# A decoder trunk on one core: the activations' blocks side by side, 16 bytes in turn, and one pass over each

## Time and profile before

| | us |
|---|---|
| median of 3 runs (lowest to highest) | 1007.06 (1006.73 to 1007.34) |
| the profiled execution | 1007.63 |
| its span, first to last instruction | 1005.8 |
| PE busy | 993.8 |
| DVE busy | 721.1 |
| ACT busy | 510.8 |
| POOL busy | 122.6 |

### The profile page before, as it was taken

The page is one execution under the profiler, slowest core; times in us unless marked ns, Lnnn a source line. Parts: engine busy times, 40 slices in busy tenths (PEclk is TensorE's granted clock), DMA queues, the critical chain, the costliest instruction groups (busy, mean ns, idle before and its releaser), DMA issues.

```text
span 1005.8 us, 19130 instructions
## 1 busy us (share of the span) xinstructions
PE 993.8 (99%) x7932; PEld 977.8 (97%) x7932; DVE 721.1 (72%) x1077; ACT 510.8 (51%) x743; POOL 122.6 (12%) x136
## 2 busy tenths in 40 slices
PE   8999999999999999999999999999999999999997
PEld 7999999999999999999999999999989999999986
DVE  5855657689899866557697565667897998866543
ACT  5643445465456543445565444445867766544340
POOL 2000002320002000003220000134152420000000
PEclk9999999999999999999999999999999999999999
DMA  9966656637762866556639665555355747866531
GB/s 249 263 194 181 176 159 179 192 93 209 232 177 81 242 199 181 168 164 183 198 89 259 179 185 156 172 168 161 85 148 145 201 116 234 254 196 197 184 132 42
DMA packets 324264, 176.60 MB, mean 176 GB/s; under 512 B 6658, under 2 KB 320048, under 8 KB 324176
## 3 DMA queue, kind: packets, MB, share of 16 engines
q1 hardware_dynamic: 323664, 174.15, 59.6%
q0 software_dynamic: 480, 1.15, 0.4%
q10 hardware_dynamic: 32, 0.07, 0.0%
HBM read 174.29 MB, written 1.05 MB: 174 GB/s over the span
## 4 chain that ended last, share of the span: by engine, by line
PE 90%; DVE 4%; DMA 1%; ACT 1%; issue 1%; POOL 1%; SPq 0%; POOLq 0%; DVEq 0%; ACTq 0%
PE bank L1318 23%; PE bank L1315 23%; PE bank L1320 23%; PE bank L1334 3%; PE bank L1335 3%; PE bank L1336 3%; PE bank L1475 2%; PE bank L1476 2%; PE bank L1474 2%; PE bank L1359 2%; PE bank L1360 2%; PE bank L1361 2%; DVE weights_lo L823 1%; DMA raw_weights<-in_ffn_w_in_dram 1%; DVE rms L1223 1%
## 5 line engine op out<-in xcount | busy, mean ns | idle before, releaser
L464 ACT ACTIVATE weights_hi<-raw_weights 128x1024 fp32r<-128x1024 f32 x335 | 353.7, 1059 | 403.9 <-PE bank L1320 286.5
L823 DVE TENSOR_TENSOR weights_lo<-raw_weights,weights_hi 128x1024 fp32r<-128x1024 f32 x334 | 417.0, 1255 | 196.0 <-ACT weights_hi L464 194.8
L1315 PE MATMUL bank<-x_hi,weights_hi 128*128 128x272 f32 (+1 forms) x1584 | 225.7, 285 | 0.5 <-ACT consts L628 0.5
L1318 PE MATMUL bank<-x_hi,weights_lo 128*128 128x272 f32 (+1 forms) x1584 | 224.0, 283 | 0.0
L1320 PE MATMUL bank<-x_lo,weights_hi 128*128 128x272 f32 (+1 forms) x1584 | 223.0, 282 | 0.0
L1315 PEld LDWEIGHTS bank<-x_hi,weights_hi 128*128 128x128 f32 x1584 | 206.0, 189 | 1.1 <-ACT consts L628 0.7
L1318 PEld LDWEIGHTS bank<-x_hi,weights_lo 128*128 128x128 f32 x1584 | 204.8, 188 | 0.0
L1320 PEld LDWEIGHTS bank<-x_lo,weights_hi 128*128 128x128 f32 x1584 | 204.2, 187 | 0.0
L1320 PE MATMUL bank<-mid_lo,weights_hi 128*128 128x272 f32 x462 | 67.2, 285 | 0.0
L1318 PE MATMUL bank<-mid_hi,weights_lo 128*128 128x272 f32 x462 | 66.8, 284 | 0.0
L1315 PE MATMUL bank<-mid_hi,weights_hi 128*128 128x272 f32 x462 | 66.7, 284 | 0.0
(11 more groups left out here) (230 smaller groups left out, 1208.6 us busy)
## 6 DMA issues: line engine op xcount, KB each, us to landing
raw_weights<-in_ffn_w_in_dram SPq DMA_DIRECT2D x176, 512.0 KB, 4.6
raw_weights<-in_ffn_w_out_dram SPq DMA_DIRECT2D x70, 512.0 KB, 3.6
raw_weights<-in_conv_w_in_dram SPq DMA_DIRECT2D x24, 512.0 KB, 3.9
raw_weights<-in_gla_w_in_dram SPq DMA_DIRECT2D x24, 512.0 KB, 3.9
raw_weights<-in_ffn_w_out_dram SPq DMA_DIRECT2D x24, 384.0 KB, 3.2
raw_weights<-in_conv_w_out_dram SPq DMA_DIRECT2D x8, 512.0 KB, 4.9
raw_weights<-in_gla_w_out_dram SPq DMA_DIRECT2D x8, 512.0 KB, 5.0
x_tok<-in_x_dram SPq DMA_DIRECT2D x2, 512.0 KB, 4.9
```

The source lines that it names most:

```text
L464: nc.scalar.activation(w_hi[:, n % RING, :], raw[:, n % RAW, :], ACT.Copy).then_inc(hi_split, 1)
L823: nc.vector.tensor_tensor(w_lo[:, s, :], raw[:, n % RAW, :], w_hi[:, s, :].bitcast(F32), ALU.subtract).then_inc(lo_split, 1)
L1315: nc.tensor.matmul(into, block_of(w_hi, n, k - k0), walk(hi[:, k, cols]), start=first and k == k0, stop=False)
L1318: nc.tensor.matmul(into, block_of(w_lo, n, k - k0), walk(hi[:, k, cols]), start=False, stop=False)
```

## The change

The four-pass walk is taken from the streamed activations, and their memory is laid out so that a single pass has the same 64-byte step. An area has groups of four blocks (SIDE = 4); in a group 4 words (RUN = 4, 16 bytes) of block 0 are followed by 4 of block 1, of block 2, of block 3, and then the next 4 of block 0. `side_by_side(area)` gives a function `block(k, cols)`, which returns block k as lines of 4 words, 64 bytes from line to line. `runs(ap)` gives a contiguous row the same shape of lines of 4, so that the two sides of an instruction agree; PSUM is then written from first to last column. The engines that write hi and lo parts write them into this layout, and with the same number of elements as before. `mid_hi` and `mid_lo` become one tensor of 44 blocks. The units with 256 columns in the GLA stage, and `y`, take the layout too. The fourth FFN keeps its packed x at the same offset of 48 words, and its middle blocks are packed at 256 words without the meta tokens (`last_mid`); the weights there are streamed by rows as before. No instruction, wait or transfer is added or removed.

```diff
+    RUN, SIDE = 4, 4
...
-        x_hi_area = sb("x_hi", [P, KD, T + 16], F32R)
-        x_lo_area = sb("x_lo", [P, KD, T + 48], F32R)
-        x_hi, x_lo = x_hi_area[:, :, 0:T], x_lo_area[:, :, 0:T]
+        x_hi_area = sb("x_hi", [P, KD // SIDE, T // RUN, SIDE, RUN], F32R)
+        x_lo_area = sb("x_lo", [P, KD // SIDE, T // RUN, SIDE, RUN], F32R)
+
+        def runs(ap):
+            return ap.rearrange("p (l e) -> p l e", e=RUN)
+
+        def side_by_side(area, first=0):
+            def block(k, cols):
+                at = first + k
+                return area[:, at // SIDE, cols.start // RUN:cols.stop // RUN, at % SIDE, :]
+            return block
...
-            mid_hi = inner.enter_context(nc.sbuf_tensor("mid_hi", [P, KF, T], F32R))
-            mid_lo = inner.enter_context(nc.sbuf_tensor("mid_lo", [P, KF, T], F32R))
+            mid = inner.enter_context(nc.sbuf_tensor("mid", [P, 2 * KF // SIDE, T // RUN, SIDE, RUN], F32R))
+        mid_hi, mid_lo = side_by_side(mid), side_by_side(mid, KF)
+        mid_words = mid[:].rearrange("p g l k e -> p (g l k e)")[:, 0:2 * KF * SEQ]
+        last_mid = mid_words.rearrange("p (s k t) -> p s k t", s=2, k=KF)
...
-                nc.scalar.activation(y_hi[:, m, :], y_t[:, m % 4, :], ACT.Copy).then_inc(yhi_ready, 1)
+                nc.scalar.activation(y_hi(m, main), runs(y_t[:, m % 4, :]), ACT.Copy).then_inc(yhi_ready, 1)
...
-                    nc.vector.tensor_copy(mid_hi[:, at_t, cols], prod[:, s:s + 1, cols]).then_inc(midhi_ready, 1)
+                    if f == 3:
+                        part_hi, part_lo = runs(last_mid[:, 0, t, :]), runs(last_mid[:, 1, t, :])
+                    else:
+                        part_hi, part_lo = mid_hi(t, cols), mid_lo(t, cols)
+                    nc.vector.tensor_copy(part_hi, runs(prod[:, s, cols])).then_inc(midhi_ready, 1)
...
-                walk = by_rows if ps.shape[-1] == T else lambda ap: ap
-                into = walk(ps)
+                into = runs(ps)
...
-                        nc.tensor.matmul(into, block_of(w_hi, n, k - k0), walk(hi[:, k, cols]), start=first and k == k0, stop=False)
+                        nc.tensor.matmul(into, block_of(w_hi, n, k - k0), hi(k, cols), start=first and k == k0, stop=False)
...
-                    nc.tensor.matmul(ps, mid_hi[:, k, toks], by_rows(w_hi[:, slot, cols]), start=False, stop=False)
+                    nc.tensor.matmul(ps, last_mid[:, 0, k, toks], by_rows(w_hi[:, slot, cols]), start=False, stop=False)
```

More of the change, by code:

```diff
@@ L79, in hybrid_trunk @@
     CLOSE_AT = 3 * LINE // 4
+    RUN, SIDE = 4, 4
+    assert T % RUN == 0 and META % RUN == 0 and KD % SIDE == 0 and 2 * KF % SIDE == 0
     ctx = ExitStack()
@@ L91, in hybrid_trunk, with block @@
         w_lo = sb("weights_lo", [P, RING, KU * P], F32R)
-        x_hi_area = sb("x_hi", [P, KD, T + 16], F32R)
-        x_lo_area = sb("x_lo", [P, KD, T + 48], F32R)
-        x_hi, x_lo = x_hi_area[:, :, 0:T], x_lo_area[:, :, 0:T]
-        def close_packed(area):
-            words = area[:].rearrange("p k t -> p (k t)")
-            return words[:, CLOSE_AT:CLOSE_AT + KD * SEQ].rearrange("p (k t) -> p k t", k=KD)
+        x_hi_area = sb("x_hi", [P, KD // SIDE, T // RUN, SIDE, RUN], F32R)
[7 more added lines that the diff above has]
+            return block
+        def close_packed(area):
+            words = area[:].rearrange("p g l k e -> p (g l k e)")[:, CLOSE_AT:CLOSE_AT + KD * SEQ]
+            def block(k, cols):
+                return runs(words[:, k * SEQ + cols.start:k * SEQ + cols.stop])
+            return block
+        x_hi, x_lo = side_by_side(x_hi_area), side_by_side(x_lo_area)
         x_close = close_packed(x_hi_area), close_packed(x_lo_area)
@@ L149, in hybrid_trunk @@
         pad_y = gb("pad_y", [P, LINE // 8])
-        y_hi = gb("y_hi", [P, KD, SEQ], F32R)
-        y_lo = gb("y_lo", [P, KD, SEQ], F32R)
+        y_hi_area = gb("y_hi", [P, KD // SIDE, SEQ // RUN, SIDE, RUN], F32R)
+        y_lo_area = gb("y_lo", [P, KD // SIDE, SEQ // RUN, SIDE, RUN], F32R)
+        y_hi, y_lo = side_by_side(y_hi_area), side_by_side(y_lo_area)
+        every, main = slice(0, T), slice(0, SEQ)
         kT = gb("kT", [P, HEADS, T])
@@ L430, in y_low @@
                 pool.wait_ge(yhi_ready, m + 1)
-                nc.gpsimd.tensor_tensor(y_lo[:, m, :], y_t[:, m % 4, :], y_hi[:, m, :].bitcast(F32),
+                nc.gpsimd.tensor_tensor(y_lo(m, main), runs(y_t[:, m % 4, :]), y_hi(m, main).bitcast(F32),
                                         ALU.subtract).then_inc(y_ready, 1)
@@ L926, in x_low @@
                     dve.wait_ge(xhi_ready, KD * (q + 1) + k + 1)
-                    nc.vector.scalar_tensor_tensor(out=out_lo[:, k, out_cols], in0=resid[:, k, cols], scalar=ln_bias_col(q, k),
-                                                   in1=out_hi[:, k, out_cols].bitcast(F32), op0=ALU.add,
+                    nc.vector.scalar_tensor_tensor(out=out_lo(k, out_cols), in0=runs(resid[:, k, cols]), scalar=ln_bias_col(q, k),
+                                                   in1=out_hi(k, out_cols).bitcast(F32), op0=ALU.add,
                                                    op1=ALU.subtract).then_inc(xlo_ready, 1)
@@ L1243, in y_low @@
                 dve.wait_ge(yhi_ready, m + 1)
-                nc.vector.tensor_tensor(y_lo[:, m, :], y_t[:, m % 4, :], y_hi[:, m, :].bitcast(F32),
+                nc.vector.tensor_tensor(y_lo(m, main), runs(y_t[:, m % 4, :]), y_hi(m, main).bitcast(F32),
                                         ALU.subtract).then_inc(y_ready, 1)
@@ L1333, in multiply @@
                     w_h, w_l = block_of(w_hi, n, k - k0), block_of(w_lo, n, k - k0)
-                    nc.tensor.matmul(into, w_h, walk(hi[:, k, cols]), start=first and k == k0, stop=False)
-                    nc.tensor.matmul(into, w_h, walk(lo[:, k, cols]), start=False, stop=False)
-                    mm = nc.tensor.matmul(into, w_l, walk(hi[:, k, cols]), start=False, stop=last and k == k1 - 1)
+                    nc.tensor.matmul(into, w_h, hi(k, cols), start=first and k == k0, stop=False)
+                    nc.tensor.matmul(into, w_h, lo(k, cols), start=False, stop=False)
+                    mm = nc.tensor.matmul(into, w_l, hi(k, cols), start=False, stop=last and k == k1 - 1)
                 mm.then_inc(unit_used, 1)
@@ L1381, in out_projection @@
             def out_projection(q, n0, k_parts, source, ready, n_tok):
-                shift_in = 0 if source[0].shape[2] == T else T - n_tok
-                src_cols = slice(tokens(n_tok).start - shift_in, T - shift_in)
+                src_cols = slice(0, n_tok)
                 cols = tokens(n_tok)
@@ L1546, in _ @@
             n0 = unit0["gla"]
-            main = tokens(SEQ)
             def logits(h):
@@ L1612, in _ @@
                 short = HEADS < j <= 2 * HEADS or j > 2 * HEADS + KD
-                cols = main if short else every
+                cols = tokens(SEQ) if short else every
                 middles = ((3, lambda: logits(1)), (6, lambda: logits(2))) if j == 5 else ()
```

40 lines of the change are left out of this document (19 added, 21 removed).

## The result

The changed kernel takes 1029.37 us (1029.21 to 1033.43, 5 runs) against 1007.34 (1006.73 to 1011.0) of the kernel before beside it: a ratio of 1.0224, 95% interval 1.0197 to 1.0251. The forecast was 1003.0 in a range of 987 to 1021. It is slower by 22.0 us, and the time lies beyond the range, on the side of rival 2. The span is 1027.6 us, 21.8 above the one before.

A forecast was written before the change was run, and what follows sets the result against it. The prediction took TensorE's matmul count times start-to-start distance as the bound; -3.3 - 0.8 + 0 + 0 = -4.1 us gave 1003.5 on the profiled execution, 1003.0 on the median, range 987 to 1021.

The forecast's parts named there:

- rival 2: One pass sits in bad places against the weight load: 11.5 to 12.8 ns excess, +9.8 to +16.8 us, about 1020; chance 0.26.
- What bounds the kernel: TensorE, busy 993.8 of 1005.8 us: time is the number of matmuls times the start-to-start distance, plus about 12 us.
- Single pass at 272 columns: 5424 matmuls on x, mid and yc: 122.4 ns each, -3.3 us, bounds -16.8 to +14.6 us.
- the rows nearest in kind: Strided rows of the old profile, with excesses of 9.7, 7.5 and 10.0 ns, mean 9.1, used to price the single pass.
- Turning from pass to pass is not what costs: Claim from the old rows: four passes at 256 columns are among the cheapest, and 512 columns' longer passes have larger excess.
- The excess as stream and weight load meeting: Time above one column a cycle was read as streamed block and next weight load meeting in SBUF, depending on relative place.
- 256 columns in GLA: 456 matmuls from x and y going from contiguous to strided: half of a 1.5 us gain, -0.8 us, worst +0.8.
- Last FFN and projection: FFN read unchanged; the projection's stationary mid blocks lie 1024 instead of 1088 bytes apart: 0, with 0.7 us either way.
- Rounding in 16-byte pieces; cover after the norms: Writes of high and low parts keep their cost and hide, with 0.55 us slack after norms: 0, at the end +3 us.
- The two rules: Skill pages on non-contiguous PSUM slowing matmuls and on independent read ports; the prediction said the profile rows spoke against both.
- Rival 1: One pass finds the good place: 120.0 to 120.8 ns a matmul, -12.5 to -16.8 us and -1.6, about 991; chance 0.27.
- The last sign I gave: Prediction wrong if single blocks in one stage differ much more than now, so one of four places carries the result.

The follow-up runs named there:

- micro5: Back-to-back matmuls on zeros alone, 64-byte steps, only the offset between passes changed: one 16-byte place visited 126.0 to 127.3 ns, two 123.7 to 125.7, four 121.4 to 122.9.
- micro2: Matmuls on zeros alone, weight block cut from 128 columns, then weights and stream shifted together: one pass 125.9, 129.4, 132.1 ns for 64, 32, 16 columns.
- micro1: Matmuls on zeros alone, read and PSUM orders compared from 16 start places: at 272 columns contiguous 125.2, four passes 121.9, one pass 126.8 ns.
- micro6: Matmuls on zeros alone, start places taken in turn from matmul to matmul: places 0 and 4 in turn, four passes, 122.8 ns.
- x_and_mid_placed: Kernel before the change, four-pass read kept, x blocks 320 words apart and 64 bytes in, middle blocks in pairs at places 0 and 4: 998.88 us, ratio 0.991.

## Why the prediction was wrong, point by point

- **What bounds the kernel.** Right. The time is the number of matmuls times the distance; the ledger above closes to 0.1 us with nothing else in it.
- **Single pass at 272 columns: the failed step.** I took 122.4 ns and bounds of 120.0 to 125.8; it is 127.1 on `x`, 126.2 on `mid` and 126.3 on `yc`, and 126.8 in the measurement alone. The term was -3.3 and came out at 14.8 + 5.5 + 0.7 = +21.0 us. Two things were wrong in it. First the mean over "the rows nearest in kind": the strided rows of before all visit the four 16-byte places in turn, which is the very thing the change takes away. I named it ("it stays in one of the four 16-byte places ... where before it took each place for 68") and let it widen the spread, but not move the mean. micro5 shows that it moves the mean by 5 ns (4.1 and 3.5 in the kernel); the error lay in the mean, not in the spread. Second the upper bound: `zg`, at 12.5 ns of excess, was the worst row in sight, not the worst there can be (and rival 2 was already priced to 12.8, beyond it). No row of before read in one 16-byte place, and single places cost up to 133.3 ns, an excess of 20.
- **"Turning from pass to pass is not what costs."** True as far as it goes: the turn costs nothing. But what the turns bring, the other places, is a gain of 5 ns, and the sentence hid it.
- **The excess as stream and weight load meeting.** The dependence on their relative place stands (micro2, last part). That less load means less loss does not. What meets what remains open.
- **256 columns in GLA.** Wrong in sign: half a gain of 3.3 ns was taken, a loss of 2.4 (`x`) and 4.0 ns (`y`) came: +1.4 us for -0.8, beyond the +0.8 that was the bound. The step is the same: one pass was priced by rows of four, 114.2 ns. micro1 has 114.9 for four passes, 117.9 contiguous and 120.4 for one pass.
- **Last FFN and projection.** The FFN stayed at 113.3 to the tenth. The projection's 512-column matmuls went up 4.1 ns, twice the spread I allowed: +0.9 for 0 ± 0.7.
- **Rounding in 16-byte pieces; cover after the norms.** Right: 303 for 302 ns and no wait on `x_lo`.
- **The two rules.** That a non-contiguous pattern in PSUM slows matmuls (the Trainium skill, "PSUM — Partial Sum Buffer", Specifications (TRN2)) was rightly not followed for pieces of 16 bytes: 1007.52 us with PSUM in order, 1007.14 beside it without. That TensorE's read ports are independent and never wait (the Trainium skill, "SBUF — State Buffer", Who interferes with whom) is spoken against by 120.0 to 133.3 ns for the same matmul at another place, while the shorter weight loads of micro2, which freed nothing, do not speak against it. The Trainium skill, "SBUF — State Buffer", Specifications (TRN2), also says that SBUF has 16-byte lines, that at least two accesses in a line are needed for full bandwidth, and that crossing to a new line costs. By that the kernel's orders, all in whole lines of four words, should cost the same, and the runs show that they don't. The 235.5 ns in 8-byte pieces can't be set against it, since PSUM was walked in 8-byte pieces too and the two were not separated.
- **The rivals.** Rival 2 happened, "the alternation that the four passes gave is gone", with 13.8 ns of excess on `x` and 12.9 on `mid` for the 11.5 to 12.8 I priced. What I held against it (its rows were unbroken reads or weights) was no argument, since an unbroken read is gentler: 125.2 in micro1, 126.8 for one pass. Rival 1 was half true: single places do run at 120.0, but no four side by side were all such a place (124.1 to 127.8 in micro6). The last sign I gave, single blocks differing by much more than now, did not show: over the eight positions of a unit on `x` the means range from 123.8 to 129.2 ns, where before they ranged from 119.0 to 127.6. The whole level rose.

## What to carry to other kernels

When TensorE is bound by the distance of its matmuls, the place of the streamed block relative to the weights matters beside its order: here every `x` block at one place modulo 256 bytes, at a cost of 1 KB a partition, gained 0.6% at place 0 and 1.0% at place 4 and lost 0.7% at place 10, while a cleaner-looking order lost 2.2%. So try the places in the kernel and not only alone; from block to block, a change of place cost 2 ns a matmul on average in micro6. And when rows near a change are averaged for its price, ask first which property they all share and the changed form lacks; that one can't be bounded by them.

## What the runs showed of the hardware

- At full clock, 272 float32 columns of 16-byte pieces often settle at a few distances, 120.0, 123.3, 126.7, 130.0 and 133.3 ns, 3.3 ns apart (and 116.7 at four places, with a narrower weight block); the others lie between. 113.3, one column a cycle, was never reached, while 256 contiguous columns took 113.3 at two places of sixteen and 117.9 in the mean.
- The step from piece to piece matters irregularly: 122.9 ns at 3 lines of 16 bytes, 127 at 4, 143.3 at 5, 173.3 at 6, 127.0 at 7, 154.1 at 16.
- PSUM's order: 122.0 against 121.9, and 126.8 against 126.8 ns.
- Open: the mechanism behind the places, why the same place settles at 120.0 ns in one measurement and at 125 to 127 in another, why place 10 is cheap alone and dear in the kernel, and why the 512-column matmuls lose 4 ns when their stationary blocks are moved (1024 bytes apart in the changed kernel, in pairs in x_and_mid_placed).
